# Bias table of an attention layer: one product of eight rows, and one transfer that repeats them

## The reference

```
bias = rel_bias[t5_bucket(jnp.maximum(delta, 0) * dilation)].astype(jnp.float32)
logits = jnp.einsum('bdhnqe,bdhnke->bdhnqk', qb, kw) + bias
logits = jnp.where(valid[None, None, None], logits, -jnp.inf)
```

## Time and profile before

| | us |
|---|---|
| median of 3 runs | 1949.16 |
| lowest, highest | 1948.77, 1949.35 |
| the profiled execution | 1946.61 |
| its span | 1944.9 |

### The profile page before, as it was taken

One profiled execution on the slowest core, in us unless ns is written; L12 is line 12 of the kernel. 1 busy time (PEld: TensorE's weight loads), 2 busy tenths in 40 slices (PEclk: granted clock), 3 DMA queues, 4 the chain that ended last, 5 costly groups with the idle time before them and its releaser, 6 DMA issues.

```text
span 1944.9 us, 27243 instructions
## 1 busy us (share of the span) xinstructions
PE 1937.1 (100%) x10846; PEld 1659.6 (85%) x10846; DVE 1379.8 (71%) x1809; ACT 952.3 (49%) x1449; POOL 523.9 (27%) x394
## 2 busy tenths in 40 slices
PE   9999999999999999999999999999999999999999
PEld 7899998877788999988999988877777888999997
DVE  8777776554588777768877776773458667877774
ACT  6555444535564445445544444443646345444542
POOL 1332222152222222223322222200015413322321
PEclk9999999999999999999999999999999999999999
DMA  6555663341336665535566653222200235666653
GB/s 214 154 163 165 182 174 98 121 173 55 89 115 191 173 170 163 161 122 148 166 175 181 176 152 121 94 95 87 76 1 1 87 109 156 189 169 170 171 158 102
DMA packets 112461, 265.81 MB, mean 137 GB/s; under 512 B 10320, under 2 KB 22864, under 8 KB 112336
## 3 DMA queue, kind: packets, MB, share of 16 engines
q1 hardware_dynamic: 92336, 225.72, 34.9%
q0 software_dynamic: 19856, 38.28, 11.5%
q10 hardware_dynamic: 144, 0.09, 0.0%
HBM read 259.32 MB, written 4.72 MB: 136 GB/s over the span
## 4 chain that ended last, share of the span: by engine, by line
PE 96%; DMA 2%; DVE 1%; issue 0%; ACT 0%; SPq 0%; POOL 0%; DVEq 0%
PE BANKS L582 11%; PE BANKS L583 11%; PE BANKS L584 11%; PE BANKS L670 10%; PE BANKS L662 7%; PE BANKS L659 7%; PE BANKS L661 7%; PE BANKS L729 6%; PE BANKS L730 5%; PE BANKS L731 5%; PE BANKS L674 5%; DMA ASR<-gu_dram 2%; PE BANKS L1042 2%; PE BANKS L870 1%; PE BANKS L872 1%; PE BANKS L871 1%
## 5 line engine op out<-in xcount | busy, mean ns | idle before, releaser
L1700 DVE TENSOR_TENSOR LO<-RING,HI 128x1024 fp32r<-128x1024 f32 (+2 forms) x204 | 227.3, 1115 | 41.0 <-ACT HI L1180 39.6
L582 PE MATMUL BANKS<-XHL,HI 128*128 128x512 f32 x624 | 245.6, 394 | 1.3 <-DVE LO L2220 1.2
L583 PE MATMUL BANKS<-XHL,HI 128*128 128x512 f32 x624 | 243.2, 390 | 0.0
L584 PE MATMUL BANKS<-XHL,LO 128*128 128x512 f32 x624 | 243.0, 389 | 0.0
L2286 POOL TENSOR_TENSOR HL<-TMP,HH 128x512 fp32r<-128x512 f32 x88 | 134.7, 1530 | 357.2 <-ACT HH L1199 357.2
L1193 ACT ACTIVATE TMP<-TMP 128x512 f32<-128x512 f32 x88 | 55.6, 632 | 304.5 <-DVE TMP L1729 304.4
L2284 POOL TENSOR_TENSOR TMP<-TMP,RSTD 128x512 f32<-128x512 f32 x88 | 131.6, 1495 | 244.4 <-ACT TMP L1193 244.4
L1180 ACT ACTIVATE HI<-RING 128x1024 fp32r<-128x1024 f32 (+2 forms) x204 | 178.8, 877 | 37.3 <-DMA RING<-down_dram 20.6
L729 PE MATMUL BANKS<-HH,DHI 128*128 128x512 f32 x488 | 191.2, 392 | 0.9 <-DVE DLO L1770 0.8
L730 PE MATMUL BANKS<-HL,DHI 128*128 128x512 f32 x488 | 190.6, 391 | 0.0
L731 PE MATMUL BANKS<-HH,DLO 128*128 128x512 f32 x488 | 189.9, 389 | 0.0
(11 more groups left out here) (258 smaller groups left out, 5108.3 us busy)
## 6 DMA issues: line engine op xcount, KB each, us to landing
RING<-gu_dram SPq DMA_DIRECT2D x174, 512.0 KB, 4.5
ASR<-gu_dram SPq DMA_DIRECT2D x146, 256.0 KB, 3.1
ASR<-gu_dram POOLq DMA_DIRECT2D x73, 512.0 KB, 6.8
DRAW<-down_dram SPq DMA_DIRECT2D x40, 512.0 KB, 4.5
RING<-oin_dram SPq DMA_DIRECT2D x32, 512.0 KB, 3.2
RING<-down_dram SPq DMA_DIRECT2D x32, 384.0 KB, 3.2
DRAW<-down_dram SPq DMA_DIRECT2D x24, 384.0 KB, 3.9
RING<-ein_dram SPq DMA_DIRECT2D x16, 512.0 KB, 3.4
```

What stands on the lines that cost most here:

```text
L582: pe.matmul(PS[bank][:], HI[j][:, c], hi(k), start=(n == 0), stop=False)
L583: pe.matmul(PS[bank][:], HI[j][:, c], lo(k), start=False, stop=False)
L584: last = pe.matmul(PS[bank][:], LO[j][:, c], hi(k), start=False, stop=(n == len(order) - 1))
L1700: dve.tensor_tensor(LO[j][:, cols], RAW[j][:, cols], HI[j][:, cols].bitcast(F32), ALU.subtract).then_inc(lo_ready, 1)
```

## The change

The sixteen products become two: the weight is now all of `RB`, eight columns, so that the result has eight rows, one for each head, and every product serves all heads at once, one for the columns 0 to 512 and one for 512 to 640. ScalarE copies two pieces of eight partitions into `STG`, now one tensor of 640 columns of which partitions 0 to 7 are used. One DMA reads each of these eight rows 128 times and writes the table of 2.62 MB. It stands behind the load of unit 7 and ahead of that of unit 8, and waits for the two copies. The wait for the table behind the load of unit 12 stays.

```diff
-        STG = [at(f"STG{n}", [P, HA // 2, BW], hr0, 8 * n * TB) for n in range(2)]
+        STG = at("STG", [P, BW], hr0, 0)
...
-        STAGED_AT = {1: range(0, 4), 3: range(4, 8), 4: range(8, 12), 5: range(12, 16)}
+        BIAS_PARTS = ((0, T), (T, BW))
...
-            for n in range(4, 11):
-                load(Q_EIN + n // 4, n % 4, ein_d[n if n < 8 else 8 + (n - 4) % 8])
-            for n in range(2):
-
-                sp.wait_ge(bias_staged, HA * (n + 1))
-                sp.dma_start(skew_d[4 * n:4 * n + 4].rearrange("h p z -> p h z"), STG[n][:]).then_inc(skew_out, 16)
-            for n in range(11, 13):
-                load(Q_EIN + n // 4, n % 4, ein_d[n if n < 8 else 8 + (n - 4) % 8])
-            sp.wait_ge(skew_out, 32)
+            for n in range(4, 8):
+                load(Q_EIN + n // 4, n % 4, ein_d[n])
+            sp.wait_ge(bias_staged, 2)
+            sp.dma_start(skew_d, STG[0:HA, :].unsqueeze(1).to_broadcast([HA, P, BW])).then_inc(skew_out, 16)
+            for n in range(8, 13):
+                load(Q_EIN + n // 4, n % 4, ein_d[8 + (n - 4) % 8])
+            sp.wait_ge(skew_out, 16)
...
-            def bias_part(n):
-
-                if n == 0:
-                    pe.wait_ge(bias_ready, 3)
-                    pe.wait_ge(std_ready, 2)
-                if n >= 4:
-                    pe.wait_ge(bias_staged, n - 3)
-                h, (z0, z1) = n // 2, ((0, T), (T, BW))[n % 2]
-                pe.matmul(PS[4 + n % 4][:, 0:z1 - z0], RB[:, h:h + 1].to_broadcast([P, P]),
-                          HOTR[:, z0:z1], start=True, stop=True).then_inc(bias_sum, 1)
+            def bias_rows():
+
+                pe.wait_ge(bias_ready, 3)
+                pe.wait_ge(std_ready, 2)
+                for n, (z0, z1) in enumerate(BIAS_PARTS):
+                    pe.matmul(PS[4 + n][0:HA, 0:z1 - z0], RB[:], HOTR[:, z0:z1], start=True,
+                              stop=True).then_inc(bias_sum, 1)
...
-                for n in range(4):
-                    bias_part(n)
+                bias_rows()
                 for j in range(SLOTS):
                     unit(q0 + 1, j, KX, xh, xl)
-                    for n in range(4 * j + 4, 4 * j + 8) if j < 3 else ():
-                        bias_part(n)
...
-                    act.activation(STG[h // 4][:, h % 4, z0:z1], PS[4 + n % 4][:, 0:z1 - z0],
-                                   ACT.Copy).then_inc(bias_staged, 1)
+                    act.activation(STG[0:HA, z0:z1], PS[4 + n][0:HA, 0:z1 - z0], ACT.Copy).then_inc(bias_staged, 1)
```

More of the change, by code:

```diff
@@ L779, in even_mixer @@
                 unit(q0, 3, KX, xh, xl)
-                for n in range(4):
-                    bias_part(n)
+                bias_rows()
                 for j in range(SLOTS):
                     unit(q0 + 1, j, KX, xh, xl)
-                    for n in range(4 * j + 4, 4 * j + 8) if j < 3 else ():
-                        bias_part(n)
                 def square_rows():
-                    pe.wait_ge(bias_staged, 2 * HA)
+                    pe.wait_ge(bias_staged, 2)
                     for n, m in enumerate((0, 1, 4, 5, 2, 3, 6, 7)):
@@ L1350, in staged @@
                 def staged(n):
-                    h, (z0, z1) = n // 2, ((0, T), (T, BW))[n % 2]
+                    z0, z1 = BIAS_PARTS[n]
                     act.wait_ge(bias_sum, n + 1)
-                    act.activation(STG[h // 4][:, h % 4, z0:z1], PS[4 + n % 4][:, 0:z1 - z0],
-                                   ACT.Copy).then_inc(bias_staged, 1)
+                    act.activation(STG[0:HA, z0:z1], PS[4 + n][0:HA, 0:z1 - z0], ACT.Copy).then_inc(bias_staged, 1)
                 for n in range(12):
@@ L1360, in even_mixer @@
                     split_unit(N_EIN + n + 4)
-                    for part in STAGED_AT.get(n, ()):
+                    for part in range(2 if n == 1 else 0):
                         staged(part)
```

## The result

The changed kernel takes 1983.1 us (median of 5 runs, 1982.8 to 1984.6), the kernel before 1948.8 us in the same session: a ratio of 1.0184, 95% interval 1.0173 to 1.0195. It is 34.4 us slower. Its profiled execution took 1984.63 us, 38.0 us more than that of the kernel before. Of 25 executions of the kernel before taken for the experiments, eleven have a mean granted clock of 1.0 and a median of 1945.8 us, and fourteen have 0.999 and 1949.4 us; its profiled execution has 1.0.

What follows compares the result with a forecast made beforehand. TensorE's unbroken row of products bounds the kernel; unit 8 waiting behind the table DMA (+32.7 us) plus restart (1.6) gives +34.3 on the median 1949.2: 1983.5 us. Own range 1977 to 1992; 8-in-10 range 1945.5 to 1992.

Steps and rivals of the forecast that it cites:

- The kernel is one row of products: TensorE, busy 1937.1 of 1944.9 us: only products taken out of its unbroken row, or holes opened in it, count.
- Products: 2.6 us saved, swallowed by the hole: TensorE's bias products: four groups cost 3.04 us, the one left 0.44; the gain lies ahead of the hole before unit 8.
- No slack lost at SyncE's wait: SyncE, between the loads of units 7 and 8: copies end about 375.6, unit 8's load goes out at 379.4 anyway.
- Loads don't pass the transfer: SyncE's queue: loads of units 8 to 11 stay behind the table DMA, each landing about 1.3 us after the DMA ahead.
- Two sixteenths, 49.9 us of payload: Table DMA from eight partitions: two of sixteen parts of the full 420 GB/s, 52.5 GB/s, for 2.62 MB.
- the bounds: Table DMA's cost: lower 6.2 us if the source doesn't limit reads, upper 99.9 us if rate follows partitions, 8 of 128.
- the step back by one doubling: Table DMA's payload: taken as 49.9 us, one doubling from the 99.9 us upper bound.
- Restart: 1.6 us: TensorE behind the hole: slow first products, as at the program's start, lose 1.6 us; at worst 0 or twice that.
- The total: Unit 8 starts 32.7 us later, with the restart +34.3 us; median 1983.5 us.
- The first rival: Table DMA: source doesn't bind (at least 210 GB/s), no hole before unit 8, 2.6 us saved, 1946.6 us; chance 0.21.
- The rival with four sixteenths: Table DMA at 105 GB/s: unit 8 at 406.2, +7.8 to +9.4 us, 1957 to 1959 us; in-between cases' chance 0.07.
- Full proportion: Table DMA at 26.25 GB/s, 8 of 128 partitions: unit 8 at 481.1, +82.7 us and restart, 2033 us; chance 0.08.

Runs made afterwards that it cites:

- the wide source: Changed kernel with the bias weight widened to 16 columns a head, so the transfer reads all 128 partitions, 8 times each: 1942.7 us, ratio 0.9975.
- the source spread out: Changed kernel with the transfer reading eight partitions four apart (0, 4 ... 28): 1944.6 us; or all 128 partitions: 1942.7 us.
- the experiment that has four groups: Changed kernel with the transfer reading eight partitions eight apart (0, 8 ... 56), each 128 times: 1958.2 us, ratio 1.0059.

## Why the prediction was right, point by point

- **The kernel is one row of products, so a hole costs its full length.** Right in kind: one wait of 38.2 us and a span 38.0 us longer. That the two agree so well is chance: the wait begins 2.6 us earlier by the products saved, so unit 8 starts only 35.8 us later than before (434.16 against 398.37), and the slow restart adds 2.8 us.
- **Products: 2.6 us saved, swallowed by the hole.** Right on both counts. Unit 8 could have started at 395.8, as worked out; the wide source shows 2.7 us with the hole gone. That a product of 8 result rows costs what one of 128 costs is now seen: with either, the two products together last 0.46 us (at 373.68 and 373.70 in the traces), and the first product of unit 4 starts 0.29 us after they do.
- **No slack lost at SyncE's wait.** Right: issue at 375.75, forecast 375.6; the load of unit 8 goes out at 379.70, forecast 379.4. What the forecast didn't have is that the issue itself then takes 17.2 us. No further wait came of it: TensorE's list has none for units 9 to 11.
- **Loads don't pass the transfer.** Right: unit 8's tile 52 us after its issue; with the transfer moved, unit 11's instead.
- **Two sixteenths, 49.9 us of payload.** The choice between the bounds was right, the price a little low: 50 GB/s and not 52.5, so 52.4 us. The tile comes at 431.8 instead of 428.7, and unit 8 starts at 434.2 instead of 431.1. The reason that I gave (half the partitions, half the rate) is not the rule, and taken at face value it gave 26.25 GB/s; that the step back by one doubling hit the right size was luck as far as the traces went. The runs give the rule: what counts is groups, not partitions; 64 partitions got half the rate because they lie in half of the groups (206 GB/s from 32 as well as from 64, 204 from eight in eight groups). The page "SBUF — State Buffer" of the Trainium skill has this rule in "Door 1: The DMA port swizzle", with the pairing of p and p + 32, and the runs agree with it: 50, 102, 204 and 206 GB/s for 2, 4, 8 and 8 of its ports, 25 to 25.8 GB/s each, where it states 27.2.
- **Restart: 1.6 us.** Mis-sized: fourteen products took 5.71 us for 13 steps where 13 x 0.227 are 2.95, so 2.8 us, within the 0 to 3.2 that I allowed. The twelve first products of the program, from which I took it, were 0.373 us apart on the average and not 0.43, so only slow in part.
- **The total.** In the clock of the profiled execution the forecast was +34.3 us and the landmark behind unit 8 moved from 403.90 to 442.53, +38.6, the span by 38.0. The medians differ by 34.4. So the sum was 4 us short, and the close agreement of the medians (1983.5 forecast, 1983.1 measured) is luck: I worked out a difference in the profiled execution of the kernel before, which lay 2.6 us below the median of 1949.2, and added it to that median, and the profiled execution of the changed kernel lay 1.5 us above its own median. The kernel before gave single times from 1944.8 to 1950.4 us over 25 runs; a forecast can't be judged here to better than that. The stated range has a slip too: a payload of 60 us and a restart of 3 us add up to 1995 us and not 1992 (the lower end, 1977, is right). The measured time lies inside either way.

The first rival needed 180 GB/s, the source as it was gave 50; with the source spread out it came true, 1944.6 and 1942.7 us, no slower than forecast (1946.6). The rival with four sixteenths came true in kind in the experiment that has four groups: 1958.2 us lies in the 1957 to 1959 worked out for it, but against the kernel before of its own session that is +11.4 us where +7.8 to +9.4 were worked out. Unit 8 started at 407.85 instead of 406.2, and the restart cost 2.8 us instead of 1.6 at most. Full proportion (26.25 GB/s) fell with the 50 GB/s of the changed kernel.

## What to carry to other kernels

A product or a copy that needs only eight rows is no cheaper on eight partitions than on 128, but a DMA out of them is slower by the groups of partitions left out (50 GB/s from two groups, 390 from all sixteen); so let the weight repeat its columns until the result covers all partitions, and send each row fewer times. Before a slow transfer is put into a queue, look at what stands behind it: here the table's readers wanted it 26 us after its issue (375.8 to 401.8), but the tile of the load behind it 18 us after (by 393.4). Another queue helps only in part: it cost 21 us instead of 36, because the loads beside the slow transfer became slow too.

## What the runs showed of the hardware that I had not expected

- One partition alone, read 128 times, gives 25.5 GB/s, as much as a whole group (eight of them 204 GB/s at 51% of the engines). With four neighbours in a group, each gets a quarter.
- A slow transfer in another queue makes loads of 512 KB land after 16.3 us instead of 3.4, though the transfer itself moves 50 GB/s and half of the engines are free.
- A slow transfer also holds up the issue of the load behind it on the same queue. That one issue took 17.2 us in the changed kernel, 15.6 us with the transfer in its old place and 7.3 us with the source of four groups, where 0.33 us is usual; each time the rate rose only when it was through (at 396.9, 412.0 and 387.0), as if the free engines had no load before that. With the transfer on the other queue the issues took 0.33 us. What the issue waits for stays open.
- The granted clock is 0.50, that is 1.2 GHz, in the hole; a hole of 11.9 us and one of 38.2 us cost the same behind it, 13 steps in 5.71 us. Behind the holes of 6.1 and 35.1 us of the other runs the slow stretch was much the same, 13 steps in 5.70 us and 14 in 6.14 us.
